# Sliding-window attention layer: two heads' scores as products of 64 rows into two PSUM banks, turned probabilities in the second output bank, one output bank

## The reference, cut to what matters

```
q, k, v, gate = split(h @ w_in)          # 16 heads, 2 kv heads, head dim 64
q, k = rope(q), rope(k)
for each block of 128 queries:           # 4 blocks
    s = q @ k.T * 64**-0.5               # keys: this block and the one before
    s = where(0 <= q_pos - k_pos < 128, s, -1e30)
    p = softmax(concat([s, sink]))[..., :-1]
    o = p @ v
out = (o * silu(gate)) @ w_out
```

## Time and profile before

| | |
|---|---|
| median of 3 runs | 2927.94 us (2924.08 to 2934.93) |
| the profiled execution's own time | 2925.89 us |
| its span, first to last instruction | 2923.9 us |
| mean granted TensorE clock | 0.969 of 2.4 GHz |
| TensorE busy | 2738.4 us, 94% of the span |
| VectorE busy | 1312.2 us, 45% |
| ScalarE busy | 658.3 us, 23% |
| GpSimd busy | 1072.0 us, 37% |
| TensorE's share of the chain that ended last | 84% |

### The profile page before, as it was taken

How to read it: one execution, slowest core, us unless ns; L and a number is a source line. 1 busy time by engine, 2 the same in 40 slices (tenths; PEclk the granted TensorE clock), 3 DMA queues, 4 the chain that set the end, 5 groups by cost and what they waited for, 6 DMA issues and landing times.

```text
span 2923.9 us, 32628 instructions
## 1 busy us (share of the span) xinstructions
PE 2738.4 (94%) x11915; PEld 1803.4 (62%) x11915; DVE 1312.2 (45%) x2671; ACT 658.3 (23%) x1577; POOL 1072.0 (37%) x574
## 2 busy tenths in 40 slices
PE   7899999999999999999988779899999999999997
PEld 5456544475555444565545475778888444788886
DVE  7233356323555642333545663544464313433554
ACT  2133133222333332232114421211100100211101
POOL 4784286068391005840881000782000782000000
PEclk7899999989999999999989989999999999999999
DMA  7343343145241113422530002453222452222221
GB/s 238 108 128 95 94 137 101 58 125 141 67 120 42 30 43 121 128 76 58 145 122 22 1 0 58 137 164 100 86 79 80 154 164 85 72 86 86 86 90 69
DMA packets 245109, 277.77 MB, mean 95 GB/s; under 512 B 41427, under 2 KB 217824, under 8 KB 244864
## 3 DMA queue, kind: packets, MB, share of 16 engines
q1 hardware_dynamic: 216000, 175.03, 19.8%
q0 software_dynamic: 28224, 100.86, 11.3%
q10 hardware_dynamic: 768, 0.30, 0.0%
HBM read 274.06 MB, written 2.10 MB: 94 GB/s over the span
## 4 chain that ended last, share of the span: by engine, by line
PE 84%; DVE 5%; DMA 3%; issue 3%; ACT 2%; POOL 1%; SPq 1%; DVEq 0%; ACTq 0%; POOLq 0%
PE psum L722 27%; PE psum L1451 25%; PE psum L916 11%; PE psum L890 3%; PE psum L1207 2%; PE psum L777 2%; PE psum L749 2%; PE psum L902 1%; PE psum L1225 1%; DMA ring<-in_ffn_w_gate 1%; PE psum L1055 1%; PE psum L1056 1%; PE psum L1350 1%; DMA ring<-in_ffn_w_up 1%; PE psum L1341 1%
## 5 line engine op out<-in xcount | busy, mean ns | idle before, releaser
L722 PE MATMUL psum<-h,ring 128*128 128x512 f32 (+1 forms) x1776 | 759.6, 585 | 5.3 <-DVE arena L2186 3.3
L649 POOL DMA_DIRECT2D ada_ring<-in_ada_w x192 | 115.2, 600 | 1331.0 <-DVEq L2242 848.1
L722 PEld LDWEIGHTS psum<-h,ring 128*128 128x128 f32 x1776 | 336.6, 192 | 388.6 <-issue 379.8
L661 POOL TENSOR_SCALAR ada_ring<-ada_ring,cond 128x1024 f32<-128x1024 f32 x168 | 480.3, 2859 | 8.4 <-POOL ada_sum L665 2.1
L665 POOL TENSOR_TENSOR ada_sum<-ada_sum,ada_ring 128x1024 f32<-128x1024 f32 x168 | 398.4, 2371 | 14.9
L916 PE MATMUL psum<-og,ring 128*128 128x512 f32 x768 | 334.3, 594 | 0.3
L1451 PE MATMUL psum<-og,arena 128*128 128x256 f32 x1152 | 258.6, 379 | 1.7 <-ACT probs L2065 1.7
L916 PEld LDWEIGHTS psum<-og,ring 128*128 128x128 f32 x768 | 144.9, 191 | 179.9 <-issue 179.9
L1451 PEld LDWEIGHTS psum<-og,arena 128*128 128x128 f32 x1152 | 218.7, 190 | 32.1 <-issue 2.4
L1451 PE MATMUL psum<-h,ring 128*128 128x256 f32 x768 | 177.3, 381 | 1.6 <-DVE mods L2240 0.9
L1688 ACT ACTIVATE probsT<-psum 128x128 f32<-128x128 f32 (+3 forms) x232 | 104.3, 450 | 297.7 <-PE psum L890 296.9
(11 more groups left out here) (363 smaller groups left out, 3667.1 us busy)
## 6 DMA issues: line engine op xcount, KB each, us to landing
ada_ring<-in_ada_w POOLq DMA_DIRECT2D x192, 512.0 KB, 4.0
ring<-in_ffn_w_gate SPq DMA_DIRECT2D x22, 1024.0 KB, 5.4
ring<-in_ffn_w_up SPq DMA_DIRECT2D x22, 1024.0 KB, 5.3
ring<-in_ffn_w_down SPq DMA_DIRECT2D x16, 1024.0 KB, 5.2
ring<-in_sc_w_in SPq DMA_DIRECT2D x12, 1024.0 KB, 5.8
ring<-in_mla_w_in SPq DMA_DIRECT2D x10, 1024.0 KB, 5.5
ring<-in_mla_w_out SPq DMA_DIRECT2D x8, 1024.0 KB, 5.1
ring<-in_swa_w_in SPq DMA_DIRECT2D x16, 512.0 KB, 5.6
```

What stands on the lines that cost most here:

```text
L649: pool.dma_start(ada_ring[:, i % 2, :], w[k * P:(k + 1) * P, first(part)]).then_inc(arrived[i % 2], n.give(f"ada_in{i % 2}", 16))
L661: step = nc.gpsimd.tensor_scalar(piece, ada_ring[:, i % 2, :], c, None, ALU.mult)
L722: m = pe.matmul(tile.at[:, part], lhs(k), rhs(k), start=(k == 0), stop=(k == K - 1))
```

## The change

The scores of a pair become two products: each head's 64 rows of queries with 64 rows of keys, each into a bank of its own (columns 0 and 512 of a buffer of two banks). Banks 2 and 3 form one buffer, banks 4 and 5 the other, so there are two score buffers (`two_banks`, lag 1) where there were three. Turned probabilities go to bank 7 (`turn_bank=OB[1]`), one unit behind the scores, and bank 6 is the only output bank (`out_banks=1`). The exponentials, the maxima and the scaling work on the same numbers of columns as before, at other addresses. The drain's seven output products stand in one step ahead of the last values. Branches for units wider than 512 columns, which no layer takes, are removed.

The hunks are in the order of the units, the banks, TensorE's stream, ScalarE's and VectorE's.

```diff
-            units.append({"pair": pair, "kv": pair // 4, "out": pair, "q": j, "width": 2 * w, "groups": [(0, w), (w, w)],
+            units.append({"pair": pair, "kv": pair // 4, "out": pair, "q": j, "width": 2 * w, "groups": [(0, w), (T, w)],
-                          "blocks": [(e * w + i * P, key, e) for e in range(2) for i, key in enumerate(keys)]})
+                          "blocks": [(e * HALF + i * P, key, e) for e in range(2) for i, key in enumerate(keys)]})
...
+        two_banks = Depth([psum[:, b:b + 2, :].rearrange("p a b -> p (a b)") for b in (2, 4)],
+                          [probs_deep[:, i, :] for i in range(2)])
...
-            def attend(units, scores, turned, values, depth=deep, inserts={}):
+            def attend(units, scores, turned, values, depth=deep, inserts={}, turn_bank=PB, out_banks=2):
-                            pe.wait_ge(S["heads_used"], n.take("heads_used"))
+                            pe.wait_ge(S["heads_used"], n.take("heads_used") + 2 - out_banks)
-                        turned(units[done], depth.probs(done), PB).then_inc(S["probsT_done"], n.give("probsT_done"))
+                        turned(units[done], depth.probs(done), turn_bank).then_inc(S["probsT_done"], n.give("probsT_done"))
...
-                    return pe.matmul(bank[:, 0:2 * w].rearrange("p (e n) -> p e n", e=2),
-                                     swa_q[:, u["pair"] % 2, u["q"] * P:(u["q"] + 1) * P],
-                                     swa_k[u["kv"]][:, :, u["keys"]:u["keys"] + w], start=True, stop=True)
+                    for e in range(2):
+                        half = slice(64 * e, 64 * e + 64)
+                        m = pe.matmul(bank[:, T * e:T * e + w], swa_q[half, u["pair"] % 2, u["q"] * P:(u["q"] + 1) * P],
+                                      swa_k[u["kv"]][half, e, u["keys"]:u["keys"] + w], start=True, stop=True)
+                    return m
...
-                    o = OB[u["out"] % 2][:, u["q"] * P:(u["q"] + 1) * P]
+                    o = OB[0][:, u["q"] * P:(u["q"] + 1) * P]
...
-                attend(swa_units(), scores, turn_blocks, values, inserts={**inserts, **drain_inserts(swa_units())})
+                drain = {len(swa_units()) + 1: [last_heads, lambda: out_part(0, range(3, KT - 1))]}
+                attend(swa_units(), scores, turn_blocks, values, depth=two_banks, inserts={**inserts, **drain}, turn_bank=OB[1],
+                       out_banks=1)
...
-                        scored = depth.bank(step) if w > T else depth.bank(step)[:, at:at + w]
+                        scored = depth.bank(step)[:, at:at + w]
-                        c = nc.scalar.activation(probsT[:, i % 2, 0:w], PB[:, 0:w], ACT.Copy)
+                    c = nc.scalar.activation(probsT[:, i % 2, 0:w], turn_bank[:, 0:w], ACT.Copy)
-                attend(swa_units(), -1.0, inserts=inserts, sink=True)
+                attend(swa_units(), -1.0, depth=two_banks, inserts=inserts, sink=True, turn_bank=OB[1])
...
-                            last = nc.vector.tensor_scalar(p[:, at:at + w], scored[:, at:at + w], row_inv[:, b, g:g + 1], None,
-                                                           ALU.mult)
+                        last = nc.vector.tensor_scalar(p[:, HALF * g:HALF * g + w], scored[:, at:at + w], row_inv[:, b, g:g + 1],
+                                                       None, ALU.mult)
-                    return nc.vector.scalar_tensor_tensor(og[:, u["pair"] * T:(u["pair"] + 1) * T], OB[u["out"] % 2], 0.5,
+                    return nc.vector.scalar_tensor_tensor(og[:, u["pair"] * T:(u["pair"] + 1) * T], OB[u["out"] % banks], 0.5,
-                       pair_out(lambda u: swa_gate[:, u["pair"] % 3, :]), inserts=inserts, sink=True)
+                       pair_out(lambda u: swa_gate[:, u["pair"] % 3, :], 1), depth=two_banks, inserts=inserts, sink=True)
```

More of the change, by code:

```diff
@@ L1660, in gate_tanh, with attend @@
                 nc.scalar.activation(dst, tile.at, ACT.Tanh, scale=0.5).then_inc(S["gate_tanh"], n.give("gate_tanh"))
-            def attend(units, scale, depth=deep, inserts={}, sink=None):
+            def attend(units, scale, depth=deep, inserts={}, sink=None, turn_bank=PB):
                 def exps(step):
@@ L2323, in maxima @@
                     dve.wait_ge(S["scores_done"], n.take("scores_done"))
[L2324 to L2328, removed]
                     if u.get("branch") == 0:
@@ L2389, in causal_mask, with pair_out @@
                 return span_mask[:, 4 * P - u["width"]:4 * P]
-            def pair_out(gate):
+            def pair_out(gate, banks=2):
                 def out(u):
-                    return nc.vector.scalar_tensor_tensor(og[:, u["pair"] * T:(u["pair"] + 1) * T], OB[u["out"] % 2], 0.5,
+                    return nc.vector.scalar_tensor_tensor(og[:, u["pair"] * T:(u["pair"] + 1) * T], OB[u["out"] % banks], 0.5,
                                                           gate(u), ALU.mult, ALU.mult)
```

## The result

| | before | after |
|---|---|---|
| median | 2927.44 us (2924.08 to 2934.93, 4 runs) | 2972.14 us (2962.61 to 2974.83, 4 runs) |
| profiled execution, span | 2923.9 us | 2970.3 us |
| mean granted clock | 0.969 | 0.965 |

The ratio after to before is 1.0143, 95% interval [1.0114, 1.0173]: slower by 1.4%. The same program, timed again on the chip of the second group of experiments, gave 1.0115 [1.0092, 1.0139]. Two of the twelve executions of e7, at 6780.22 and 5690.57 us, were in a slow state and are left out of its ratio; all others were fast.

What follows compares the result with a forecast made beforehand. TensorE's own work was taken to bound the sliding layer, softmax hidden beneath it. Blocks A 2.1 + 5.7, blocks B 12.0, drain 6.4 and GpSimd 4.5 made 30.7 us: 2959 us, 1.05% slower, range 2948 to 2970.

Steps and rivals of the forecast that it cites:

- Edit 2, the ring: Two score buffers: softmax of successive units becomes one serial chain over VectorE and ScalarE, 3.71 us for a full unit.
- Blocks A: TensorE from query product's end to gate product's start: 5.66 us, 0.95 above 4.71 six times, 2.07 above 3.59 once.
- blocks B: TensorE's stretch from the gate product's end to the next query product: 5.75 us, 2.0 above 3.74, six times 12.0.
- Edit 1, the scores: Scores as 64-row products: a full unit 0.54 us, saving 0.32; about 8 us in all, hidden under a wait.
- rival (a): Two units in flight suffice and the scores' 8 us saving arrives: not slower, 2920 us; chance 0.07.
- Edit 3, one output bank: Turns in bank 7, one output bank: values wait for the previous pair's evacuation, which is covered; costs nothing.
- Edit 4, GpSimd: GpSimd holds up VectorE's row sums, now in the ring, in nine blocks: 0.5 us each, 4.5 us.
- The drain: The layer's end, opened by the seventh block B: nothing hides the ring, 26.5 us against 20.1, +6.4.
- rival (b): TensorE's clock falls in the drain, its seven products at 1.2 GHz take 6 us more: 2965 us; chance 0.13.

Runs made afterwards that it cites:

- e7: The kernel of e6 with the sinks' part of the row sums added by scalar operands; ratio 1.0012 to the kernel before.
- e1: The kernel before with two one-bank score buffers in place of three in the sliding layer, and the changed kernel's drain; ratio 1.0110 to the kernel before.
- e9: The changed kernel with the edits of e3 and e4 together; ratio 1.0106 to the kernel before, layer 200.8 us.
- e5: The changed kernel with scores, exponentials and maxima ahead of the inserts within a step; ratio 1.0046 to the kernel before.
- e2: The changed kernel with scores as two products of 128 rows, each into its own bank; ratio 1.0121 to the kernel before.
- e8: The kernel of e7 with scores as two products of 128 rows, each into its bank; ratio 1.0014 to the kernel before.
- e3: The changed kernel with filler products, their results unused, ahead of values that wait on TensorE; ratio 1.0100 to the kernel before.
- e4: The changed kernel with the sinks' part added to the row sums by two scalar-operand instructions in place of one two-input instruction; ratio 1.0125 to the kernel before.
- e6: The kernel of e5 with the drain's seven output products spread over its last four steps; ratio 1.0032 to the kernel before.

## Why the prediction was right, and where it was short

It said 2959 us, 1.05% slower, between 2948 and 2970; measured were 2972.14 us and 1.43%, 2 us beyond the upper end, and 1.15% on another chip. The way and the main mechanism were right; one term, the clock, was mis-sized. That the time comes so near to the range owes something to luck: the range was widened for a clock that falls in the drain, and most of what the clock cost fell in the blocks' products, which had no such term. Its 0.91 for slower also does not follow from its parts, which add up to 0.93.

- **Edit 2, the ring.** Right in mechanism and size. Blocks A without a held sum took 5.61 us at the full clock (predicted 5.66), blocks B 5.71 (5.75). Had all been so, blocks A would have cost 7.5 us (7.8 predicted) and blocks B 11.8 (12.0). e1 shows that the two buffers do it alone, e9 that the ring alone, less its second sum instruction, is 25.5 us (26.2), and e5 that what costs is the ring's start behind the evacuation.
- **Edit 1, the scores.** A full unit took 0.63 us, not 0.54, so about 1.36 times as fast as 0.86 and not twice. That it arrives nowhere was right (e2). What the prediction lacked is that even uncovered it hardly arrives, because the passage into 64-row scores and out of them costs 0.20 us for each 0.23 saved. That is shown in the order of e7 (e8). By it rival (a), 2920 us, would have had little to gain; no run has the old ring with 64-row scores, so that it could not have come about is argued and not shown.
- **Edit 3, one output bank.** Its wait is not seen: e1, with two banks, is as slow.
- **Edit 4, GpSimd.** Nearly right in size: three blocks B had sums of 1.57, 1.52 and 1.90 us, two blocks A 0.51 and 0.43, together 5.1 us above 0.17 each, where 4.5 was predicted. That the ring would fall into step with GpSimd and wait 0.6 each time was wrong; most blocks had none.
- **The drain.** 27.8 us against 26.5; its seven products took 7.2 in place of 6.0, since they began at 1.2 GHz (the granted clock was 0.50 from 570 to 576 us, 0.67 from 576 to 580), and the values and turns just ahead of them 2.2 in place of 1.2.
- **The clock.** This is the step that was mis-sized: rival (b) priced it at 6 us in the drain, with 13%, and let the blocks have none, with the argument that "the gaps are under 3 us each". The gaps were as predicted, 2.0 us, but they were enough: the products lost 13.3 us (1.9 of it the first, which stands ahead of the ring), the turns in the blocks 2.0, the drain's products 1.2. e3 shows that filling the waits takes this loss away, e1 that it needs no 64-row product. The rows of before that I had for the clock were from another layer, and I weighed the drain against them but not the forecast blocks.

Later stages were as long as before (span +46.4 us, layer +47.4), as predicted.

What stays open: why one idle stretch is followed by a slow product and another is not. Over the five traces with two buffers, the old order within a step and unfilled waits (after, its repetition, e1, e2, e4) 26 of the 30 products behind a block B were slow and 3 of the 35 behind a block A. A block B has 2.0 us of idle in one piece, an undisturbed block A two pieces of 0.8 and 0.6. But a block A with a piece of 1.78 us in the repetition was followed by a product of 6.88 us, and the 2.02 us ahead of the layer's first product by a slow one in some runs and not in others. The number of slow products differs between executions of one program; no run here took that apart. And no version beat the kernel before: e7 and e8 are level with it.

## What to carry to other kernels

A second buffer does not make a pipeline by itself: ask behind which instruction of its engine each stage of the next unit stands. If the first stage of softmax stands behind the evacuation of a long product, the whole chain (3.7 us here) is exposed once a product; started ahead of the product it is hidden (undisturbed blocks of 4.43 and 3.94 us in e5, 4.71 and 3.74 in the kernel before, 5.61 and 5.71 in the changed one). And price a wait on TensorE with the clock behind it: 2 us of idling cost up to 1.7 us more in the product that followed, and 2.1 behind a block with a held sum.

## What the runs showed of the hardware that I had not expected

- Idle stretches of 2.0 us between dense products were followed by products that ran for a part at 1.2 GHz (8.58 us for 6.88; granted clock 0.57 from 510 to 514 us, 1.00 after). Slow were eight of 14 products in one execution of the program and seven in another; with the waits filled it was one, in e3 behind an idle stretch of 2.55 us, in e9 the first product, ahead of any filler.
- 64-row products between 128-row ones cost 0.20 us a passage, 0.1 going in and 0.1 coming out (7.08 against 6.88 for the product behind them, in the chain).
- Two 64-row products of 256 columns into two banks take 0.63 us, where one 128-row product of 512 columns takes 0.86.
- A row sum with the second addend as a scalar operand is not held up by GpSimd (at most 0.214 us in 64), with it as a second tensor it is, for up to 1.9 us in the changed kernel and 2.4 in e6.
